# Two transformer blocks on one core: new start addresses (homes) for the split weights in SBUF

## The reference, cut to what matters

```python
proj = u @ w_in[l]
q, k, v, cf_val, cf_gate, sc_x, sc_bg, sc_cg, gates = jnp.split(proj, SPLIT_IDX, axis=-1)
...
x = x + merged @ w_o[l]
hf = rms_norm_2(x, ffn_norm_g[l]) @ w_ffn_in[l]
gt, up = jnp.split(hf, 2, axis=-1)
x = x + (jax.nn.silu(gt) * up) @ w_ffn_out[l]
```

## Time and profile before

| what | value |
|---|---|
| median of 3 runs | 752.0 us |
| the profiled execution's own time | 750.54 us |
| its span (first to last instruction of the program) | 748.8 us |
| TensorE matmul busy | 733.3 us, 98% |
| TensorE weight load busy | 621.5 us, 83% |
| VectorE busy | 535.7 us, 72% |
| ScalarE busy | 380.2 us, 51% |
| GpSimd busy | 27.8 us, 4% |
| HBM read | 144.68 MB, 195 GB/s over the span |

### The profile page before, as it was taken

The page is one execution under the profiler, slowest core; times in us unless marked ns, Lnnn a source line. Parts: engine busy times, 40 slices in busy tenths (PEclk is TensorE's granted clock), DMA queues, the critical chain, the costliest instruction groups (busy, mean ns, idle before and its releaser), DMA issues.

```text
span 748.8 us, 11626 instructions
## 1 busy us (share of the span) xinstructions
PE 733.3 (98%) x4703; PEld 621.5 (83%) x4703; DVE 535.7 (72%) x743; ACT 380.2 (51%) x577; POOL 27.8 (4%) x44
## 2 busy tenths in 40 slices
PE   5999999999999999999999999999999999999998
PEld 3687886478888877789999999999988888888886
DVE  1486769648887898875789999647963868668431
ACT  2564567545354758445534444698443543544330
POOL 3000000001000000023000000000000000000000
PEclk9999999999999999999999999999999999999999
DMA  9994447924667343453744644513453654453711
GB/s 368 423 391 167 183 169 275 423 119 140 232 228 271 113 159 124 141 208 113 281 170 169 216 179 170 194 60 120 165 207 127 226 225 145 192 215 142 262 56 57
DMA packets 21956, 146.47 MB, mean 196 GB/s; under 512 B 2588, under 2 KB 2716, under 8 KB 5392
## 3 DMA queue, kind: packets, MB, share of 16 engines
q1 hardware_dynamic: 20880, 142.62, 51.2%
q0 software_dynamic: 752, 2.06, 0.9%
q10 hardware_dynamic: 272, 1.05, 0.3%
HBM read 144.68 MB, written 1.05 MB: 195 GB/s over the span
## 4 chain that ended last, share of the span: by engine, by line
PE 59%; ACT 0%; DVE 0%; issue 0%
PE banks L466 14%; PE banks L468 14%; PE banks L467 14%; PE banks L545 8%; PE banks L546 5%; PE banks L547 1%; PE banks L576 1%; PE banks L957 0%; PE banks L942 0%; PE banks L972 0%; PE banks L961 0%; PE banks L959 0%; PE banks L947 0%; ACT L1656 0%; PE banks L713 0%; ACT HBOTH L1227 0%
## 5 line engine op out<-in xcount | busy, mean ns | idle before, releaser
L1727 DVE TENSOR_TENSOR WL<-RAW,WH 128x2048 fp32r<-128x2048 f32 (+1 forms) x103 | 233.7, 2278 | 49.2 <-ACT WH L1209 48.7
L1209 ACT ACTIVATE WH<-RAW 128x2048 fp32r<-128x2048 f32 (+1 forms) x103 | 195.6, 1906 | 54.6 <-PE banks L468 41.0
L466 PE MATMUL banks<-HBOTH,WH 128*128 128x256 f32 x480 | 136.6, 285 | 0.0
L468 PE MATMUL banks<-HBOTH,WL 128*128 128x256 f32 x480 | 135.8, 283 | 0.0
L467 PE MATMUL banks<-HBOTH,WH 128*128 128x256 f32 x480 | 135.8, 283 | 0.0
L466 PE MATMUL banks<-WH,HBOTH 128*128 128x512 f32 (+1 forms) x320 | 127.2, 398 | 1.9 <-DVE HBOTH L1959 0.9
L468 PE MATMUL banks<-WH,HBOTH 128*128 128x512 f32 (+1 forms) x320 | 124.3, 388 | 0.0
L467 PE MATMUL banks<-WL,HBOTH 128*128 128x512 f32 (+1 forms) x320 | 124.1, 388 | 0.0
L466 PEld LDWEIGHTS banks<-HBOTH,WH 128*128 128x128 f32 x480 | 92.0, 192 | 1.1 <-issue 1.0
L467 PEld LDWEIGHTS banks<-HBOTH,WH 128*128 128x128 f32 x480 | 92.0, 192 | 0.1
L468 PEld LDWEIGHTS banks<-HBOTH,WL 128*128 128x128 f32 x480 | 92.0, 192 | 0.0
(11 more groups left out here) (305 smaller groups left out, 1004.7 us busy)
## 6 DMA issues: line engine op xcount, KB each, us to landing
RAW<-in_weights_dram SPq DMA_DIRECT2D x114, 1024.0 KB, 4.9
BIG<-in_weights_dram SPq DMA_DIRECT2D x6, 1024.0 KB, 6.5
ROTS<-in_weights_dram SPq DMA_DIRECT2D x4, 1024.0 KB, 7.5
PROBS<-in_weights_dram SPq DMA_DIRECT2D x2, 1024.0 KB, 12.1
RAW<-in_weights_dram SPq DMA_DIRECT2D x2, 816.0 KB, 10.8
GATE<-in_weights_dram SPq DMA_DIRECT2D x3, 512.0 KB, 10.3
X<-in_x_dram ACTq DMA_DIRECT2D x1, 1024.0 KB, 5.6
QT<-in_weights_dram SPq DMA_DIRECT2D x1, 1024.0 KB, 13.3
```

Of the source, the lines that this page charges most:

```text
L466: pe.matmul(out_, lhsT=w[0], rhs=x[0], start=start, stop=False, **more)
L468: return pe.matmul(out_, lhsT=w[1], rhs=x[0], start=False, stop=stop, **more)
L1209: do(act.activation(WH[:, home[n], 0:kb * width], RAW[:, slot[n] % RAW_RING, 0:kb * width], ACT.Copy), high_done)
L1727: do(dve.tensor_tensor(WL[:, home[n], w], RAW[:, slot[n] % RAW_RING, w], WH[:, home[n], w], ALU.subtract), low_done)
```

## The change

The ring of four homes becomes one flat area in each of `WH` and `WL`, with room for four pieces and 128 bytes more for each. A home has two start addresses, one for weights that move and one for weights that stand still. `place` chooses: every "cols" piece is placed at the standing one in both parts; of `fi2` to `fi10` the high part is at the standing one and the low part at the moving one; all else (rows, `fi0`, `fi1`) is at the moving one. In bytes from the start of `WH` or `WL`, the moving starts are 0, 8448, 16,640 and 25,088 (0, 256, 256, 0 modulo 512), the standing ones 64, 8256, 16,704 and 24,896 (64, 64, 320, 320 modulo 512). `WH` and `WL` grow by 512 bytes each. `ONES` (512 bytes) goes: `QUADS` is set to one by POOL once both matmuls of `gate_rows(0)` are done, and `gate_rows(1)` reads it. With that `WH` begins at 43,008, `WL` at 76,288, `HBOTH` at 117,760, all multiples of 512, and everything after them moves by 512 bytes. No matmul, copy, subtraction or DMA is added or removed, and the orders of all engines but POOL are as before.

```diff
+LINE = 16
+MOVING_AT = tuple(s * (PIECE + 2 * LINE) + (0, 2 * LINE)[s % 2] for s in range(SPLIT_RING))
+STILL_AT = tuple(s * (PIECE + 2 * LINE) + (LINE, -LINE)[s % 2] for s in range(SPLIT_RING))
+SPLIT_SIZE = SPLIT_RING * (PIECE + 2 * LINE)
...
-        QUADS, ONES, NM = sb("QUADS", [P, P]), sb("ONES", [P, P]), sb("NM", [P, n_units, 2])
+        QUADS, NM = sb("QUADS", [P, P]), sb("NM", [P, n_units, 2])
...
-        WH, WL = sb("WH", [P, SPLIT_RING, PIECE], F32R), sb("WL", [P, SPLIT_RING, PIECE], F32R)
+        WH, WL = (sb(n, [P, SPLIT_SIZE], F32R) for n in ("WH", "WL"))
...
+        def place(n, low):
+
+            name, _, _, _, kind = pieces[n]
+            if name[:2] == "fi":
+                still = not low and int(name[2:]) >= 2
+            else:
+                still = kind == "cols"
+            return (STILL_AT if still else MOVING_AT)[home[n]]
+
+        def part(n, low, w=slice(0, None)):
+
+            at = place(n, low)
+            first, last, _ = w.indices(pieces[n][2] * pieces[n][3])
+            return (WH, WL)[low][:, at + first:at + last]
...
-            _, _, kb, w, _ = pieces[n]
-            return [t[:, home[n], 0:kb * w].rearrange("p (k c) -> p k c", k=kb) for t in (WH, WL)]
+            return [part(n, low).rearrange("p (k c) -> p k c", k=pieces[n][2]) for low in range(2)]
+
+        def both_halves(name):
+
+            first = place(index[(name, 0)], 0)
+            pitch = place(index[(name, 1)], 0) - first
+            start = min(first, SPLIT_SIZE - 2 * pitch)
+            views = [w[:, start:start + 2 * pitch].rearrange("p (u c) -> p u c", u=2) for w in (WH, WL)]
+            at = lambda k: first - start + k * 256
+            return [[view[:, :, at(k):at(k) + 256] for view in views] for k in range(KB)]
...
-                sums = (QUADS, ONES)[layer]
...
-                    mm = pe.matmul(bank[:, :], lhsT=sums[:, :], rhs=ACC[:, (4 + c) * 512:(5 + c) * 512],
+                    mm = pe.matmul(bank[:, :], lhsT=QUADS[:, :], rhs=ACC[:, (4 + c) * 512:(5 + c) * 512],
...
-            pool.memset(ONES[:, :], 1.0).then_inc(ones_set, 1)
...
                     ps.wait_filled(pool, "gate0.1")
+                    pool.memset(QUADS[:, :], 1.0).then_inc(ones_set, 1)
                     clear_rows(1)
...
-                        do(dve.tensor_tensor(WL[:, home[n], w], RAW[:, slot[n] % RAW_RING, w], WH[:, home[n], w],
+                        do(dve.tensor_tensor(part(n, 1), RAW[:, slot[n] % RAW_RING, w], part(n, 0),
                                              ALU.subtract), low_done)
```

More of the change, by code:

```diff
@@ L1031, in hidden_tokens @@
                     wait_parts(pe, f"fi{i}", half)
-                slot_ = home[index[(f"fi{i}", 0)]]
+                w = both_halves(f"fi{i}")
                 use = f"fh.{i}.{t}"
@@ L1039, in hidden_tokens @@
                     mm = product(out_, [h[:, k, t * P:(t + 1) * P] for h in (HH, HL)],
-                                 [w[:, slot_:slot_ + 2, k * 256:(k + 1) * 256] for w in (WH, WL)], k == 0, k == KB - 1)
+                                 w[k], k == 0, k == KB - 1)
                 ps.fill(mm, use)
@@ L1208, in highs @@
                         continue
-                    do(act.activation(WH[:, home[n], 0:kb * width], RAW[:, slot[n] % RAW_RING, 0:kb * width], ACT.Copy),
+                    do(act.activation(part(n, 0), RAW[:, slot[n] % RAW_RING, 0:kb * width], ACT.Copy),
                        high_done)
@@ L1260, in first_highs @@
                 w = slice(part_ * kb * width // 2, (part_ + 1) * kb * width // 2)
-                do(act.activation(WH[:, n, w], RAW[:, slot[split_pieces[n]] % RAW_RING, w], ACT.Copy),
+                do(act.activation(part(split_pieces[n], 0, w), RAW[:, slot[split_pieces[n]] % RAW_RING, w], ACT.Copy),
                    (first_high, high_done)[part_])
@@ L2024, in first_lows @@
                 w = slice(part_ * kb * width // 2, (part_ + 1) * kb * width // 2)
-                do(dve.tensor_tensor(WL[:, n, w], RAW[:, slot[split_pieces[n]] % RAW_RING, w], WH[:, n, w], ALU.subtract),
+                piece = split_pieces[n]
+                do(dve.tensor_tensor(part(piece, 1, w), RAW[:, slot[piece] % RAW_RING, w], part(piece, 0, w), ALU.subtract),
                    (first_low, low_done)[part_])
```

## The result

| | before | changed |
|---|---|---|
| median of 5 runs | 752.0 us (750.4 to 752.41) | 747.6 us (746.74 to 748.82) |
| ratio | 1 | 0.9948 (0.9932 to 0.9965) |
| profiled execution | 750.54 us, span 748.8 | 746.74 us, span 745.0 |

A second comparison on another chip gave 0.9931 (0.9915 to 0.9947). So the change makes the kernel faster by 0.5 to 0.7%, 4.4 to 5.7 us, where 9.5 were forecast. 747.6 us lies inside of the range of 727 to 755, but in the first comparison less than half of the forecast gain came.

What follows compares the result with a forecast made beforehand. TensorE, busy 98% of the span, was taken to bound the kernel through start-to-start distances of matmuls. Column pieces 7.8 us and both form 1.7 us gave 9.5 us less, 752.0 to 742.5 us, range 727 to 755.

Steps and rivals of the forecast that it cites:

- rows, ring and `ONES` nothing: Rows-form matmuls, shifted starts for ScalarE and VectorE, and the memset moved on POOL: each taken at no gain or loss.
- The rival of a fixed price: All matmuls: the extra 13.3 ns is the price of changing weights, so addresses do nothing; 752 us, chance 0.24.
- the term of the column pieces: 36 pieces, 1728 matmuls of 256 moving columns: 8.6 us less, of which 7.8 kept as on the path.
- the half-way gain of 5 ns: Column pieces: 5 ns less a matmul from 120, between a fall to 109 and a loss of 4 ns.
- The full 10.9 ns of the bound: Column pieces: the most each matmul could fall, from 120 to the transposes' 109 ns; 18.8 us in all.
- The both form: 288 pairs of a 512-column and a 256-column matmul: 6 ns less a pair, 1.7 us.
- The row taken for it: Both form: one early block's trace row, 349 ns a pair against 353, taken as nearest to a better case.
- The further 2 ns for the 256 alone: Both form: gain of the 256-column matmul added to the 349 row; together 6 ns a pair.
- The rows form at nothing: Rows-form matmuls: no gain, as 512 columns pass every residue and undo a 256-byte shift; bounds 2.6 us either side.
- VectorE as the next bound: Taps: VectorE next late at 5.37 us a piece; its 6.0 us lead barely covers TensorE coming 5.0 us earlier.
- all of the extra went: Rival: columns form 109 ns, both form 325 a pair, up to 5 us wait at the taps; about 727, chance 0.22.
- The slower rival: Column pieces and both form's high weights: being off the multiples of 512 costs 4 ns; about 758 us, chance 0.16.

Runs made afterwards that it cites:

- e2: Changed kernel with every piece at the moving start, leaving the flat ring, shifted later tiles and one tile of ones; ratio to before 0.9995 (0.9981 to 1.0008).
- e1: Separate kernel without the reference: only blocks of the three forms, at varied start addresses, 0 to 6 transposes ahead; columns form 113.3 to 120.0 ns a matmul.
- e8: Changed kernel with the low part of column pieces and the high part of `fi2` to `fi10` at 192 bytes past a multiple of 256; 742.11 us, ratio to before 0.9867.
- e4: Changed kernel with only the high parts of `fi2` to `fi10` at the standing start, all else at the moving one; ratio to before 0.9982 (0.9963 to 1.0001).
- e3: Changed kernel with `fi2` to `fi10` at the moving start in both parts, other column pieces still at the standing one; ratio to before 0.9942 (0.9922 to 0.9961).
- e6: Changed kernel with one more transpose ahead of `scx`, its result overwritten; 745.76 us, ratio to before 0.9914 (0.9897 to 0.9931).
- e5: Separate kernel without the reference: chains of columns blocks behind a rows block and 0 to 4 transposes, then pairs of standing starts; columns blocks 113.3 to 118.9 ns a matmul.
- e7: Changed kernel with two more transposes ahead of `scx`; 744.76 us, ratio to before 0.9901 (0.9886 to 0.9917).

## Why the prediction was wrong

**Right: what bounds the kernel, and where to look.** The change acts through the distances between starts alone, the columns form is where the gain is, both form second, and rows, ring and `ONES` nothing (e2). The rival of a fixed price is out, and so is what it drew from a page, that no address can matter: the Trainium skill, "TensorE: Matmul & The Clock Gate", Part 2, step 1, has two independent read ports and no cost of a load for the running matmul, but here 64 bytes in the start of the standing weights change the distance from 120 to 113.3 or 117.8 ns.

**Wrong: the term of the column pieces.** The step was "I take the half-way gain of 5 ns, 1728 x 5 = 8.6 us", of which 7.8 were kept. Measured were 121.3 to 118.2 in the mean, 3.1 ns, 5.4 us. Of the 5.1 us that lack in the first comparison, 2.4 are this term, 0.7 the both form, and 2.0 what came back elsewhere, which the sum had at nothing (in the two profiles 2.5 us, 1.6 of it by the clock). The half-way value stood for a stream that is partly relieved everywhere. What there is instead are two steady rhythms, 6.7 and 2.2 ns below 120, and 24 of 36 pieces were in the poorer one, with the 17 blocks in a row that hold nearly half of the matmuls (816 of 1728) among them. Nothing in the column pieces of before shows them, as at its addresses all four entries of e1 give 120. With nearly all matmuls in the better rhythm (e8) the columns form gives 9.2 us, more than the 8.6 of the step. The full 10.9 ns of the bound were never reached at any start tried: 113.3 is the lowest.

**The both form:** 1.7 us were forecast and 1.0 came (e4 against e2), 353 to 349 ns a pair. The row taken for it gave the right distance by luck: it is one early block at the old addresses, with no start off the multiples of 512, while 349 is now the mean of blocks of 2.74, 2.82 and 2.80 us. The further 2 ns for the 256 alone weren't there.

**The rows form at nothing** was right (283.3 us before, 283.5 in e3, which has no drop), but not for the reason given. That 512 columns pass every residue doesn't make the start indifferent: at 64 and 128 bytes e1 has 228.7 and 231.9 ns. A shift of 256 bytes is free because 256 bytes are the period.

**The clock wasn't in the sum.** The profiled execution of before does have the full clock, but the earlier trace rows can't show it: a 9 is 90% or more, and the changed kernel's page has the same forty nines with a drop of 3.4 us in it. The 1.5 us between the profiled execution and the median, which the sum left unexplained, fit one such drop to 1.2 GHz. Some executions have one and some have two, behind stretches with matmuls of 2 columns (160.7 us) or 15 (109.6 us). It takes back about 1 us of the change's gain.

**VectorE as the next bound** was named rightly, and the wait in the wrong place. I expected it at the end of the taps if all of the extra went; it is at the entry of `g0`, for the draining of `sbg`'s bank, 0.6 to 0.9 us, and only once the stretch runs at 113.3 (e6 to e8). The taps stay ahead. The slower rival was right for the rows form only, where being off the multiples of 256 costs 1.5 to 6.1 ns in e1, be it with the moving operand or with the standing one. In the columns form being off gains, with either operand.

## What to carry to other kernels

In a stream with a weight load for every matmul, place the tiles and measure by start-to-start distances: in float32r, moving operands at multiples of 256 bytes, standing ones at 64 past one for the high and 192 past one for the low part, took 256-column matmuls from 120 to 113.3 ns. For 512-column ones leave both operands at multiples of 256: a standing start 64 bytes past one took them from 227 to 233. Such a stream has steady rhythms that are chosen at its entry and kept until the next wait or the next block of another form, so look at whole pieces rather than at a mean, and prefer addresses at which the slower one was not seen to a lucky lead-in. When runs fall into steps, look at each one's granted clock before reading 1 us into a median, and count the drops of both kernels: they can be a part of the change's price.

## What the runs showed of the hardware that was not expected

- The same 48 instructions at the same addresses take 5.65 or 5.44 us, by how they are entered: with 0 or 2 transposes behind a rows block the one, with 1, 3 or 4 the other (e5), and in one place with no change ahead of them at all (`z1_0`, the changed kernel against e6). The whole kernel was 2 to 3 us faster with two useless transposes in it (e7 against the changed kernel).
- The period of the standing operand's start is 256 bytes (0 and 64 floats alike, 16 and 80, 32 and 96); for the moving one 0 and 64 floats are alike, and other pairs weren't tried. 16-byte and 32-byte offsets of the standing operand give no single steady distance: 118.3 in the mean, single ones from 115 to 123. The same offsets of the moving operand alone give 116.7 in the mean.
- Why the rhythms exist, and what in the hardware ties them to the addresses, was not tried and stays open. No run leaves the loads out, so that it is the load which meets the stream is argued, not shown. Shown is that the starts matter, and that with some of them the entry, down to a few nanoseconds, goes with the rhythm.
